# Four input products of a decoder layer as seven Strassen products each, with operand sums on GpSimd

## The reference

```python
z = _rmsnorm(x, norm1_w) @ w_in      # [256,1024] @ [1024, 3592]
qa, ka, va, gate_a, beta_l, alpha_l, qb, kb, vb = _split_columns(z)
# a: gated delta network (GDN), 4 heads x 128: conv + silu of qa,ka,va, L2 norm,
#    chunked triangular solve, times silu(gate_a)
# b: dilated sliding window attention (SWA), 8 heads x 64:
#    RMS norm of qb and kb per head, scores, softmax, times vb
h   = x + concat(a, b) @ w_out       # w_out [1024,1024]
out = h + MoE(RMSNorm(h))            # top 4 of 32 experts, 12 MiB of weights each
```

## Time and profile before

| what | us |
|---|---|
| median of 3 runs | 1093.65 (1092.68 to 1095.74) |
| the profiled execution | 1093.17 |
| its span, first to last instruction | 1091.4 |
| PE busy in the span | 1026.1 |
| DVE, ACT, POOL busy | 281.6, 163.0, 14.0 |
| mean granted clock of TensorE | 0.991 |

### The profile page before, as it was taken

One profiled execution on the slowest core, in us unless ns is written; L12 is line 12 of the kernel. 1 busy time (PEld: TensorE's weight loads), 2 busy tenths in 40 slices (PEclk: granted clock), 3 DMA queues, 4 the chain that ended last, 5 costly groups with the idle time before them and its releaser, 6 DMA issues.

```text
span 1091.4 us, 12589 instructions
## 1 busy us (share of the span) xinstructions
PE 1026.1 (94%) x5004; PEld 430.2 (39%) x5004; DVE 281.6 (26%) x673; ACT 163.0 (15%) x275; POOL 14.0 (1%) x34
## 2 busy tenths in 40 slices
PE   8999999999999999989999998888999898898898
PEld 7855667333434343434344323232333332232232
DVE  3754564412222222222222110111111111111111
ACT  3503255110000000000100000000000000000001
POOL 3001000000000000000000000000000000000000
PEclk9999999999999999999999999999999999999999
DMA  9578279899999999999999999999999999999997
GB/s 317 123 243 315 78 275 357 357 427 429 426 426 432 428 434 429 431 430 428 434 425 428 429 431 429 434 435 425 430 432 431 429 431 431 431 432 434 423 424 290
DMA packets 39027, 427.62 MB, mean 392 GB/s; under 512 B 8243, under 2 KB 10516, under 8 KB 20052
## 3 DMA queue, kind: packets, MB, share of 16 engines
q1 hardware_dynamic: 37732, 426.63, 94.0%
q10 hardware_dynamic: 1264, 0.56, 0.2%
HBM read 424.42 MB, written 2.75 MB: 391 GB/s over the span
## 4 chain that ended last, share of the span: by engine, by line
PE 50%; DMA 41%; DVE 5%; ACT 2%; issue 1%; SPq 1%; ACTq 0%; DVEq 0%
DMA store<-in_w_gate_up_dram 24%; PE bank L2126 17%; DMA store<-in_w_down_dram 16%; PE bank L2182 13%; PE bank L1639 5%; PE bank L1646 3%; PE bank L2032 2%; PE bank L1894 2%; PE bank L1734 2%; PE bank L2097 1%; DVE flow L1492 1%; PE bank L2147 1%; DVE flow L1485 1%; ACT flow L930 1%; DMA brt<-in_b_router_dram 1%
## 5 line engine op out<-in xcount | busy, mean ns | idle before, releaser
L2126 PE MATMUL bank<-store,flow 128*64 128x512 f32 x2048 | 452.1, 598 | 13.7 <-DMA store<-in_w_gate_up_dram 12.8
L2126 PEld LDWEIGHTS bank<-store,flow 128*64 128x64 f32 x2048 | 146.0, 138 | 313.9 <-issue 290.8
L2182 PE MATMUL bank<-store,flow 128*64 128x512 f32 x992 | 227.0, 607 | 32.9 <-DMA store<-in_w_down_dram 21.4
L1485 DVE TENSOR_SCALAR flow<-bank 128x512 f32<-128x512 f32 x32 | 22.1, 692 | 607.4 <-PE bank L2126 607.4
L2182 PEld LDWEIGHTS bank<-store,flow 128*64 128x64 f32 x992 | 73.7, 139 | 165.5 <-issue 135.9
L930 ACT ACTIVATE flow<-flow 128x512 f32<-128x512 f32 x32 | 20.2, 630 | 444.9 <-DVE flow L1485 444.9
L2041 PE MATMUL bank<-qkT 64*128 64x512 f32 x248 | 61.9, 616 | 0.0
L1639 PE MATMUL bank<-store 128*128 128x512 f32 x128 | 57.0, 594 | 0.0
L946 ACT COPY qkT<-bank 128x512 f32<-128x512 f32 x31 | 18.1, 585 | 194.3 <-PE bank L2182 194.3
L940 ACT COPY flow<-flow 128x512 f32 x30 | 33.7, 1123 | 27.5 <-DVE flow L1560 11.2
L2041 PEld LDWEIGHTS bank<-qkT 64*128 64x128 f32 x248 | 21.3, 186 | 40.1 <-issue 40.1
(11 more groups left out here) (346 smaller groups left out, 600.4 us busy)
## 6 DMA issues: line engine op xcount, KB each, us to landing
store<-in_w_gate_up_dram SPq DMA_DIRECT2D x50, 4096.0 KB, 26.9
store<-in_w_down_dram SPq DMA_DIRECT2D x57, 2048.0 KB, 20.7
store<-in_w_gate_up_dram SPq DMA_DIRECT2D x26, 2048.0 KB, 14.5
store<-in_w_in_dram SPq DMA_DIRECT2D x6, 2048.0 KB, 14.8
store<-in_w_down_dram SPq DMA_DIRECT2D x9, 1024.0 KB, 25.0
store<-in_w_out_dram SPq DMA_DIRECT2D x1, 4096.0 KB, 13.0
store<-in_w_gate_up_dram SPq DMA_DIRECT2D x4, 1024.0 KB, 6.5
flow<-in_w_down_dram SPq DMA_DIRECT2D x1, 2048.0 KB, 12.3
```

Of the source, the lines that this page charges most:

```text
L1485: dve.tensor_scalar(gt, bank[4][:], LIMIT, None, ALU.min).then_inc(g_min, 1)
L2126: ins = mm(dst[SLOTS * hf:SLOTS * (hf + 1), :], rows[:, c:c + SLOTS], store[:, slot_at(j, odd) + c0:slot_at(j, odd) + c0 + 512], start=fir ...
L2182: ins = mm(dst[SLOTS * hf:SLOTS * (hf + 1), :], turned[:, c:c + SLOTS], w[:, hf * 512:(hf + 1) * 512], start=f == 0, stop=f == KT - 1)
```

## The change

Each late piece j (3 to 6) is computed as seven products of quarters instead of eight. x is split in two by tokens and in two by the inner dimension, the piece in two by the inner dimension and in two by columns. Every one of the seven is four products of 128x256, eight instructions. Four sums of parts of x (`s1` to `s4`, once) and four of parts of the weights (for each piece) are made by GpSimd, 128x1024 elements each. Running sums stay in a PSUM bank (`so_far`): ACT copies it out after each step (`evac_part`), PE adds on, and DVE adds a product kept apart in another bank (`apart`) to what ACT copied. The steps are `a` (two products), `b` (two), `c`, `d`, `e` (one each). The order text is rewritten around them, the squares are taken in the order 1, 3, 0, 2 after the weight sums of piece 5, and `wout`, whose slots hold sums of weights until then, is issued after `e5`. The first expert's tiles 3, 0, 1, 2 wait for `e3`, `e4`, `e5`, `e6`.

```diff
-RING = [1, 0, *range(2, 12), "f0", "f1", "f2", "f3"]
-LATE_UNITS = {12: 7, 13: 4, 14: 4}
+FIRST_UNITS = [1, 0, *range(2, 7)]
+PRODUCT_BANK = {3: (7, 5), 4: (3, 6), 5: (6, 5), 6: (4, 5)}
+SUMMED, ALL_SUMMED = {3: 3, 4: 4, 5: 5, 6: 7}, {3: 3, 4: 4, 5: 6, 6: 8}
+SQUARED = (1, 3, 0, 2)
-    text = ("01 11 z7 y8 y9 y10 z8 J0 12 z9 02 1E y11 0E 07 z10 n0 17 z11 f0 f1 f2 08 f3 y12 S0 z12 09 P0 S1 "
-            "0A y13 T0 P1 0B O0 z13 S2 0Q T1 y14 P2 0C O1 S3 1K 0M T2 P3 z14 s0 S4 O2 18 T3 P4 W0 0N T4 19 O3 "
-            "0D 1A O4 S5 P5 1B W1 T5 1Q O5 1C X0 X1 W2 w0 1M A0 1N H0 H1 1D R0 L0 W3 F0 X2 G0 M0")
+    text = ("01 11 a3 a4 b3 b4 c3 c4 J0 d3 12 d4 02 e3 0E r0 e4 1E r1 r2 n0 a5 07 17 f0 b5 f1 f2 08 f3 c5 S0 "
+            "09 d5 P0 S1 0A P1 T0 e5 S2 0B a6 O0 0Q P2 b6 0C T1 S3 c6 O1 1K T2 d6 P3 0M e6 O2 s0 S4 P4 18 T3 "
+            "0N W0 T4 19 O3 1A 0D S5 1B P5 O4 W1 T5 1Q O5 1C X0 X1 w0 W2 1M A0 1N H0 H1 R0 1D L0 W3 F0 X2 G0 "
+            "M0")
...
+        W_SUMS = {3: REST + 4 * SLOT, 4: REST + 4 * SLOT + 3072, 5: REST + 7 * SLOT, 6: END}
...
-            sp.dma_start(wout, w_out[0].rearrange("(k p) n -> p k n", p=P)).then_inc(ld_wout, 16)
-            for i in (3, 0, 1, 2):
-                sp.wait_ge(z_psum, 2 * (3 if i == 3 else 4 + i) + 3)
+            for i, j in ((3, 3), (0, 4), (1, 5), (2, 6)):
+                sp.wait_ge(z_psum, z_count("e", j))
+                if j == 5:
+                    sp.dma_start(wout, w_out[0].rearrange("(k p) n -> p k n", p=P)).then_inc(ld_wout, 16)
                 sp.dma_start(tile_dst(i), expert_tile(slice(0, 1), i)).then_inc(ld_tile[i], 16)
...
+            pool.wait_ge(xnT_ready, 2)
+            s1, s2, s3, s4 = x_sums
+            st.step(pool.tensor_tensor(s1, x_part(1, 0), x_part(1, 1), ALU.add))
+            st.step(pool.tensor_tensor(s2, s1, x_part(0, 0), ALU.subtract))
+            pool.tensor_tensor(s3, x_part(0, 0), x_part(1, 0), ALU.subtract)
+            pool.tensor_tensor(s4, x_part(0, 1), s2, ALU.subtract)
+            def weight_sums(j):
+                pool.wait_ge(ld_win[j % 4], 16 * (j // 4 + 1))
+                b11, b12, b21, b22 = quarters(j)
+                t1, t2, t4 = w_sums(j)
+                st.step(pool.tensor_tensor(t1, b12, b11, ALU.subtract))
+                st.step(pool.tensor_tensor(t2, b22, t1, ALU.subtract))
+                ins = pool.tensor_tensor(b12, b22, b12, ALU.subtract)
+                if j < 5:
+                    ins = pool.tensor_tensor(t4, b21, t2, ALU.subtract)
+                summed.mark(ins)
+            def last_sum(j):
+                pool.wait_ge(z_psum, z_count("a", j))
+                summed.mark(pool.tensor_tensor(b21, b21, w_sums(j)[1], ALU.subtract))
...
+            weight_sums(3)
+            weight_sums(4)
+            weight_sums(5)
+            for i, u in enumerate(SQUARED):
+                square(i, u)
+            last_sum(5)
+            weight_sums(6)
+            last_sum(6)
...
+            def evac_part(kind, j):
+                act.wait_ge(z_psum, z_count(kind, j))
+                dst = z_part(j, *{"a": (0, 0), "b": (0, 1), "c": (1, 1), "d": (1, 0)}[kind])
+                z.mark(act.copy(dst, product_bank(j)[1]))
...
+                if kind in "ade":
+                    apart, _ = product_bank(a)
+                    dve.wait_ge(z_psum, z_count({"a": "a", "d": "b", "e": "e"}[kind], a))
+                    dve.wait_ge(z_evac, evacuated({"a": "a", "d": "c", "e": "b"}[kind] + str(a)))
+                    part = z_part(a, *{"a": (0, 0), "d": (1, 1), "e": (0, 1)}[kind])
+                    zs.mark(dve.tensor_tensor(part, part, apart, ALU.add))
...
+            def split_product(dst, xs, ws, start=False):
+                for k in range(KT // 2):
+                    ins = mm(dst, xs[:, k, :], ws[:, k, :], start=start and k == 0, stop=k == KT // 2 - 1,
+                             skip_group_check=True)
+            def split_step(kind, j):
+                if kind == "a":
+                    pe.wait_ge(ld_win[j % 4], 16 * (j // 4 + 1))
+                    split_product(so_far, x_part(0, 0), b11, start=True)
+                    ins = split_product(apart, x_part(0, 1), b21, start=True)
+                elif kind == "b":
+                    pe.wait_ge(xnT_ready, SUMMED[j])
+                    pe.wait_ge(z_evac, evacuated(f"a{j}"))
+                    split_product(so_far, s2, t2)
+                    pe.wait_ge(z_sum, sums_done("a", j))
+                    ins = split_product(apart, s1, t1, start=True)
+                elif kind == "c":
+                    pe.wait_ge(z_evac, evacuated(f"b{j}"))
+                    ins = split_product(so_far, s3, t3)
+                elif kind == "d":
+                    pe.wait_ge(xnT_ready, ALL_SUMMED[j])
+                    pe.wait_ge(z_evac, evacuated(f"c{j}"))
+                    ins = split_product(so_far, x_part(1, 1), t4)
+                else:
+                    pe.wait_ge(z_sum, sums_done("d", j))
+                    ins = split_product(apart, s4, b22)
```

More of the change, by code:

```diff
@@ L90 @@
 BANK4_STAGES = {2, 8, 9}
-BANK4 = [step for step in ORDER if (step[0] == "gdn" and step[2] in BANK4_STAGES)
-         or (step[0] == "z" and LATE_UNITS.get(step[1]) == 4)]
-BANK7 = [step for step in ORDER if step[0] in "TO" or (step[0] == "z" and LATE_UNITS.get(step[1]) == 7)]
+BANK4 = [step for step in ORDER if (step[0] == "gdn" and step[2] in BANK4_STAGES) or step[:2] == ("a", 6)]
+BANK7 = [step for step in ORDER if step[0] in "TO"]
 def stage_counts(stages):
@@ L107, with z_count, sums_done @@
 GDN_SEQ = [(t, s) for kind, t, s in ORDER if kind == "gdn"]
+EVACUATIONS = FIRST_UNITS + [x[0] + str(x[1]) for x in ORDER if x[0] in "abcdf"]
+Z_STEPS = [("z", u) for u in FIRST_UNITS] + [x[:2] for x in ORDER if x[0] in "abcde"]
 def evacuated(user):
-    return (RING + list(LATE_UNITS)).index(user) + 1
+    return EVACUATIONS.index(user) + 1
 def z_bank(user):
-    return LATE_UNITS[user] if user in LATE_UNITS else 5 + RING.index(user) % 3
+    return 5 + FIRST_UNITS.index(user) % 3
+SUMS = [x[:2] for x in ORDER if x[0] in "ade"]
+def z_count(kind, a):
+    return Z_STEPS.index((kind, a)) + 1
+def sums_done(kind, a):
+    return SUMS.index((kind, a)) + 1
 class Tally:
@@ L399, in piece, with quarters, x_part, z_part @@
             return store[:, at:at + 2 * SLOT].rearrange("p (k n) -> p k n", n=512)
+        def quarters(j):
+            w = piece(j)
+            return [w[:, KT // 2 * kh:KT // 2 * (kh + 1), S * c:S * (c + 1)] for kh in range(2) for c in range(2)]
+        def x_part(t, kh):
+            return xnT[:, KT // 2 * kh:KT // 2 * (kh + 1), t * P:(t + 1) * P]
+        def z_part(j, t, c):
+            return (zswa[:, 2 * (j - 3) + t] if j < 6 else gate[:, t])[:, S * c:S * (c + 1)]
+        def w_sums(j):
+            at = [store[:, W_SUMS[j] + 1024 * i:W_SUMS[j] + 1024 * (i + 1)].rearrange("p (k n) -> p k n", n=S)
+                  for i in range(3)]
+            return at if j < 5 else at[:2] + [quarters(j)[2]]
+        def product_bank(j):
+            apart, so_far = PRODUCT_BANK[j]
+            return bank[apart][:, 0:S], bank[so_far][:, 0:S]
         def heads(ap, h=HG):
@@ L1219, in _ @@
                     continue
[L1220 removed]
+                if kind in "bcsfWXLTRF":
                     continue
@@ L1633, in unit @@
                 j, half = divmod(u - 1, 2)
-                pe.wait_ge(ld_win[j % 4], 16 * (j // 4 + 1))
+                pe.wait_ge(ld_win[j], 16)
                 w = piece(j)
-                if j >= 3:
-                    for k in ks:
-                        ins = mm(dst[:], xnT[:, k, half * P:(half + 1) * P], w[:, k, :],
+                for c in range(2):
+                    c0 = (2 * half + c) * P
+                    for k in range(KT):
+                        ins = mm(dst[:, c * S:(c + 1) * S], w[:, k, c0:c0 + P], xnT[:, k, :],
@@ L1640, in unit @@
                                  start=k == 0, stop=k == KT - 1)
-                else:
-                    for c in cs:
-                        c0 = (2 * half + c) * P
-                        for k in range(KT):
-                            ins = mm(dst[:, c * S:(c + 1) * S], w[:, k, c0:c0 + P], xnT[:, k, :],
-                                     start=k == 0, stop=k == KT - 1)
-                if ks[-1] == KT - 1 and cs[-1] == 1:
-                    z.mark(ins)
+                z.mark(ins)
@@ L1839, in _ @@
                     continue
-                if kind in "snwARGPJ":
+                if kind in "abcde":
+                    split_step(kind, a)
+                    continue
+                if kind in "snwARGPJr":
                     continue
```

118 lines of the change are left out of this document (71 added, 47 removed).

## The result

| | before | changed |
|---|---|---|
| median | 1093.67 (1092.68 to 1095.74, 6 runs) | 1102.71 (1100.26 to 1103.56, 6 runs) |
| profiled execution, its span | 1093.17, 1091.4 | 1100.26, 1098.5 |
| expert 0 starts on PE | 191.17 | 198.16 |
| stage 08 starts on PE | 102.16 | 112.54 |

The ratio is 1.0073, 95% interval 1.0062 to 1.0084: slower, by 6.8 to 9.2 us, and above the range given. The profiled execution of the changed kernel was its fastest, so the traces explain 7.1 of the 9.0 us between the medians; for the other 1.9 there is no trace. 08 comes 10.4 us later, the shorter products behind it give 3.4 back, expert 0 comes 7.0 later and the span ends 7.1 later. So the place to look at is PE before 08. One correction to the text on the change: the sums of x are of 128x512 elements each, not 128x1024; only those of the weights are 128x1024.

A forecast was written before the change was run, and what follows sets the result against it. PE in the front was taken to set the start of a full weight stream. -6.5 (saving) + 5.7 (places 1, 3 and 4) + 0.3 (new groups) = -0.5, giving 1093.1 us; range 1087.5 to 1099.0.

The forecast's parts named there:

- What bounds the kernel: Whole kernel: expert stage is a full weight stream from 200 us, its start set by PE in the front.
- What PE saves: Late pieces on PE: 224 instructions of 0.2175 us replace 128 longer ones, 6.7 us saved, 6.5 at the front's end.
- New groups and the copies beside PE: Late steps on PE: starting new groups costs 0.3 us (2 for the range), ACT's copies and DVE's additions nothing.
- Place 1: 16 to 25 us: sums of x on GpSimd hold DVE's first convolution, gate sums come late, PE loses 1.5 us.
- Place 2: 31.5 to 41 us: piece 3's sums meet the second and third convolutions; price 0, PE waits 4.2 if all caught.
- Place 3: 65 to 81 us: piece 4's sums delay `b4`, piece 5's hold DVE's inversion until 87.1; PE 3.9 late.
- Place 4: 91 to 108 us: GpSimd sums meet the norm's four scales on DVE; 08 is 4.9 to 9.2 late, 5.7 taken.
- GpSimd wins the handovers: Rival, second convolution and scales: the sum goes first when a DVE instruction also waits; +4.3, 1098.0 us, chance 0.22.
- The engines share without loss: Rival, DVE beside GpSimd: no holding, only piece 4's late landing (1.7) remains; -4.8, 1088.9 us, chance 0.30.
- the change doesn't save on PE: Rival, late products: short instructions run slower than 0.2175 us, at 0.25 the saving is gone; 1099.7 us, chance 0.04.
- slower: Total time: slower than before by more than 0.3%, 3.3 us; chance 0.25.

## Why the prediction was wrong

**The account.** In terms of expert 0's start: before 191.17; the kernel without any sum -3.3; all sums but those beside the scales +2.1; sums beside the scales +8.2; together 198.16. The -3.3 holds the late piece 4 of that one execution; by the estimate above the first two terms are rather -5.4 and +4.2, and their sum is the same. The prediction had -6.5 + 5.7 + 0.3.

- *What bounds the kernel*: right. Expert 0 later by 7.0, span longer by 7.1, DMA share 1.0 behind it.
- *What PE saves*: right in its size and pace (0.2175 forecast; 32 instructions in 7.21 us are 0.225 with the last one's end, 72 are 0.219). Of the 3.4 us behind 08 all arrived.
- *New groups and the copies beside PE*: 0.3 forecast. Between the three waits no step on PE waits 0.2 us or more, so nothing visible.
- *Place 1* (1.5 us): wrong. I took the sums of x for 128x1024; they are 128x512, 1.27 to 1.33 us each, ended at 21.3, and the first convolution began at 22.0. PE began the gate's sums at 26.02, before its 26.51.
- *Place 2* (0): right. Piece 3's sums stretched the third convolution and a tiny gate instruction (0.15 to 2.05 us), nobody on PE waited. Its price in a worse order was seen in the experiment with piece 4 earlier.
- *Place 3* (3.9 with place 1): the mechanism came as told and nearly to the moment. `b4` at 74.47 (74.1; the sums took 2.34 to 2.42 us each, forecast 2.2), the inversion's end at 87.68 (87.1). It reached PE not at `e3` but one step earlier, at the turn `02`, whose result DVE takes out of PSUM behind the inversion: 2.44 + 3.17 = 5.6. That is 1.7 too little.
- *Place 4*: this is the step that failed. Its part of the 5.7 was 5.7 - 3.9 = 1.8, the bounds 1.0 and 5.3; measured 6.20 of wait and 1.55 of clock between 07 and 08, 8.1 by where 08 stood (112.54 - 96.09 less 8.4 without stalls), and 8.2 by the experiment. All waits together made 08 13.4 late (112.54 against 99.1), and -6.5 + 13.4 is the +7.0 seen but for 0.1. Two errors are in it.

The first is how I chose between the ends: from one meeting, where L1270 got its turn right behind a single square, I took it that a handover lets several through. But a single meeting with one GpSimd instruction and nothing behind it cannot tell that; each scale but the first, which met the rest of one, waited for a whole sum (9.62 us in all, which is the bad end of my range). And the waits of a sum for the one before left DVE a gap of only 0.08 us (102.05 against 101.97), time for one scale to begin and not for two.

The second is why even the bad end, 08 at 108.3, was too early by 4.2. I let only the copies of 07 and 17 stand behind the scales. DVE's queue there also holds the addition of `a5`, and `b5`'s second product on PE waits for it, ahead of `f1`, `f2` and 08. So what comes after the scales is not one copy but a product step of 1.89 us and the turns; and PE, idle for 6.2 us, ran that step at a lower clock, of which no term spoke ("no term below hangs on it").

**The rivals.** *GpSimd wins the handovers* was the nearest: its point of decision, 08 later than 105.7, was passed, its bad end for the scales came true, and its 1098.0 was 2.3 under the profiled execution and 4.7 under the median. It was wrong in two things: its remainder of place 2 (1.6) did not come, and its price of place 4 lacked the queue on DVE and the clock. *The engines share without loss* is refuted by the scales, 684 to 2822 ns, and *the change doesn't save on PE* by the pace. The chance of "slower" was 0.25; the bad end of place 4 was the plain reading of the rule that place 1 had already drawn (the second stands until the first has ended). But even with it the sum is -6.5 + 9.2 + 0.3 = +3.0, that is 1096.7, 6.0 under the median and less than the 3.3 us that the prediction took for clear. The rest is the second error, the queue on DVE and the clock.

**What stays open.** The 1.9 us between the medians that the profiled execution doesn't show. How much of the lateness in the kernel without sums belongs to the sums' absence. And the granted clock near 75 us: in the changed kernel the wait of 2.44 us for `b4` is followed by 32 instructions in 7.17 us, in two of the experiments (sums behind the norm, squares on ACT) waits of 2.47 and 2.13 by the same 32 in 8.86 us, at a granted clock of 0.83 between 74 and 84. In the first of the two nothing of it reaches 07, since PE then waits 1.56 us instead of 3.17 behind the inversion. What decides between full and lower clock was not tried.

## What to carry to other kernels

Work given to an idle GpSimd is not free if it reads SBUF and DVE has instructions with two SBUF inputs on the path: count one GpSimd instruction's time for each such DVE instruction (in the inversion, with instructions of 0.2 us, for every second one), and everything queued behind it on DVE with those who wait for it. Put such sums where DVE's next instructions are waited for by nobody, or take other work off GpSimd so that its sums have room to move (here the squares, to ACT); the same saving on PE that lost 0.7% then won 0.5%. And when the nearest row shows one meeting of two instructions, read from it how long one waits, not how many pass.

## What the runs showed of the hardware that I had not expected

- Of instructions as long as the scales one gets in at the end of each sum. Four scales take 9.62 us in the changed kernel, 7.80 beside the four shorter sums in the kernel before, 5.39 beside sums of half the length, and 0.68 each beside memsets. Of the inversion's tiny ones two got in at the end of a sum: the held one ended at 79.23, and a second began at 79.27, just ahead of the next sum (79.29), and took its 0.17.
- Instructions with one tensor in SBUF are held as well: the copy at the head of the inversion took 1.02 us at 75.94, beside a sum, and 0.37 before; and a float32 `tensor_scalar` of 0.35 us took 2.50. Its line in the changed kernel (ns, least, median, most; 12 instructions, one group met piece 3's sums):

```profile
L1164 DVE TENSOR_SCALAR flow<-store,cw x12: 345/348/2503, 21.4 to 58.1; 128x256 f32<-128x256 f32 x12
```

I had reckoned with two inputs only. The same section of the Trainium skill, "SBUF — State Buffer", "Who interferes with whom", counts `tensor_scalar` among those that can take the shared pair in a two-port mode, and this row agrees.
- The granted clock falls in the front of the kernel after 6.2 us of idle PE and costs 1.55 us on top of the idle time, and after 5.1 and 5.4 us in the two kernels with piece 4 earlier, where it costs 2.0 and 2.6. After 2.13 and 2.47 us it fell in two traces; after 2.03, 2.44 and 3.17 us it did not. It fell as well after 0.83 and 1.65 us close together, beside the sums in the kernel before.
